# Two-layer hybrid decoder step: panel tiles in pieces, products without a reader, an opening on halves

## The chip, the cores and the metric

The kernel runs on one core of one Trainium2 chip. The metric is the device time of one execution in microseconds (us), median of three runs.

## The reference, cut to what matters

Two layers, 256 prompt tokens and 32 sample tokens (8 sequences of 4) with the same weights, all in float32. Each layer projects x (288 tokens x 1024) on 3592 columns, gives them to four recurrent head groups (RG-LRU, mLSTM, retention, HGRN2, 4 heads of 64 each), and projects their outputs back:

```python
proj = einsum('btd,de->bte', x, w_in[l])               # 14 groups of 256 columns and 8 gate columns
ya, yb, yc, yd = rglru(..), mlstm(..), retention(..), hgrn2(..)   # chunked recurrences, new states
x = layer_norm(ALPHA * x + concat(ya, yb, yc, yd) @ w_out[l])
# layer 0: swiglu, 1024 -> 2816 -> 1024; layer 1: top 2 of 8 experts, 1024 -> 1408 -> 1024
x = layer_norm(ALPHA * x + ffn(x))
```

The outputs are x of both groups of tokens and all new states.

## The kernel before, in words

The kernel is one program of five instruction streams, each written out by hand in its order, tied by semaphores. x lies in SBUF transposed, 8 blocks of 128 channels x 288 tokens. A **panel** is 256 columns of a weight matrix (1 MB), loaded by SP's queue into one of eleven slots; w_in has 14 panels a layer, which alternate between slots 0 and 1. A panel gives two **tiles** of 128 columns x 288 tokens; a tile is 8 products of TensorE (one for each block of channels) that accumulate in bank 0 or 1 of PSUM. Each float32 product has two records in the trace.

A **mixing stage** (`mix(l)` in TensorE's stream) computes the 28 tiles in the order FD QD KB QB XA VB KC QC ID VC GA GD GC OB. Between the tiles stand the small products of the four head groups: gate rows, the eight levels of HGRN2 (`level`), decays, scores, `outputs` (64-column heads, and one product of 4 columns for each sample sequence and head, `carried`), prompt states and sample states, means and variances of heads. ScalarE copies each tile out of PSUM (`in_ev`), VectorE computes the recurrences' elementwise parts in its own fixed order, and a `need(name, step)` lets an engine wait for a named step of another. Banks 2 and 3 (`A_`), 4 and 5 (`B_`), 6 and 7 (`C_`) are shared by the small products. Of the names that come up later: `m5`, `l6` are merge 5 and the operands of level 6 on VectorE, `ml_dv y` is its copy of mLSTM's outputs with the three operations behind it, `hg_dv y` and `ret_dv y` the same for the others; GpSimd spreads the values for the sample states (`vm_ready`).

**The opening** (layer 0). SP's queue loads the gate weights, x's first half (blocks 0 to 3), panel 0, x's second half, small tables, panel 1, large tables. GpSimd's queue loads the columns (small vectors), the LRU weights and three states. TensorE runs the gate products, tile 0, gate rows, tile 1. VectorE computes constants from the columns (lines 1553 to 1584), then copies the gate products (line 1912) and goes on with `gate_bias`, `forget` and so on to the operands of level 0.

**After the second mixing stage** stands the routing: layer norm of x in two halves of tokens (`mean`, `variance`), the products of the router (`logit_parts`), transposes of x to rows (`x_rows`), selection of experts on VectorE, positions of the tokens (products with `before` and `ones`), and `first_tokens`, which gathers the first expert's tokens by one-hot products. Then each of the 8 experts has an up part (16 steps over W1 and W3, 384 records) and a down part (264 records).

Line 583 is `mm`, the helper of all products, 586 is `tr`, a transpose as a product with the identity; 1286 is the helper of all of ScalarE's operations.

## Time and profile before

| what | value |
|---|---|
| median of 3 runs | 1114.41 us (1111.52 to 1116.57) |
| the profiled execution | 1113.72 us |
| its span, first to last instruction | 1111.9 us |
| mean granted clock of TensorE | 0.969 |
| TensorE matmul / weight load busy | 1071.3 / 758.2 us |
| VectorE / ScalarE / GpSimd busy | 324.0 / 170.2 / 74.7 us |
| HBM traffic | 228.60 MB read, 13.07 MB written |

By stages, in us from the span's start: opening to 22, mixing stage of layer 0 to 194, output projection and dense feed-forward to 505, mixing stage of layer 1 to 678, output projection and routing to 744, experts to 1095, combination and last norm to the end. A view in order of time merges instructions of one kind that follow each other: start, time, engine, line, operation, output <- inputs, rows x columns, number, and in brackets how long the engine had been idle before and what ended that. Busy times of TensorE are those of a pipeline: the differences of starts are used for what a piece of work takes.

### The profile page before, as it was taken

To read this page: it belongs to the slowest core of one execution; us is meant where nothing else is said; L and a number is where in the kernel's file an instruction comes from. 1 tells how busy PE (TensorE), PEld (TensorE's weight loads), DVE (VectorE), ACT (ScalarE), POOL (GpSimd) and SP (SyncE) were. 2 spreads that over 40 slices of the span, in tenths; PEclk is the share of its full clock that TensorE was granted. 3 is DMA by queue.
4 is the path that set the end of the run, shared out by engine and by line. 5 is a ranking of instruction groups with operands and counts; after the bars stand their busy time and mean duration, and the time that the engine had idled before them with its cause. 6 is when DMAs were issued, how large, how long until landed. Compare 5 with 4: busy or idle time off the path is not lost.

```text
span 1111.9 us, 20901 instructions
## 1 busy us (share of the span) xinstructions
PE 1071.3 (96%) x9627; PEld 758.2 (68%) x9627; DVE 324.0 (29%) x686; ACT 170.2 (15%) x360; POOL 74.7 (7%) x94
## 2 busy tenths in 40 slices
PE   6999999999999999999999999889999999999995
PEld 4787766897777777897876766733566566566552
DVE  4645535240000000137546443441110110110116
ACT  1322223130000000024222222220000000000011
POOL 1000113000000000000010300030000020000001
PEclk9998999999999999999998989959999999999998
DMA  8342147303433612403422335769999999999944
GB/s 340 114 190 77 39 135 261 152 11 142 151 151 124 263 49 104 185 1 104 185 92 75 101 119 230 281 228 385 363 402 418 401 409 397 423 421 423 408 151 131
DMA packets 36252, 240.06 MB, mean 216 GB/s; under 512 B 4736, under 2 KB 8064, under 8 KB 16320
## 3 DMA queue, kind: packets, MB, share of 16 engines
q1 hardware_dynamic: 26608, 216.40, 49.5%
q0 software_dynamic: 6416, 19.52, 5.1%
q10 hardware_dynamic: 3136, 2.75, 0.8%
q8 instruction: 77, 1.26, 0.5%
q14 instruction: 15, 0.12, 0.0%
HBM read 228.60 MB, written 13.07 MB: 217 GB/s over the span
## 4 chain that ended last, share of the span: by engine, by line
PE 94%; DVE 3%; ACT 1%; DMA 1%; issue 1%; SPq 0%; DVEq 0%
PE ps L583 93%; PE ps L586 1%; DMA x<-in_x 1%; ACT overlay L1286 1%; ACT L1286 0%; DVE overlay L1620 0%; DVE up_slots L1720 0%; ACT up_slots L1286 0%; DVE tables L2136 0%; DVE overlay L2019 0%; DVE up_slots L1959 0%; DVE up_slots L1713 0%; DVE up_slots L1960 0%; DVE tables L2143 0%; ACT x L1286 0%
## 5 line engine op out<-in xcount | busy, mean ns | idle before, releaser
L583 PE MATMUL ps<-x,up_slots 128*128 128x288 f32 (+2 forms) x1696 | 411.1, 402 | 0.9 <-ACT x L1286 0.8
L583 PEld LDWEIGHTS ps<-x,up_slots 128*128 128x128 f32 x1696 | 314.3, 194 | 89.4 <-issue 8.4
L583 PE MATMUL ps<-up_slots,mix_or_moe 128*32 128x352 f32 (+2 forms) x3248 | 253.0, 458 | 2.9 <-issue 1.6
L583 PEld LDWEIGHTS ps<-up_slots,mix_or_moe 128*32 128x32 f32 (+2 forms) x3248 | 126.5, 113 | 119.7 <-issue 25.6
L583 PE MATMUL ps<-overlay,up_slots 128*128 128x288 f32 (+2 forms) x824 | 150.9, 344 | 2.7 <-DVE overlay L2052 1.5
L583 PEld LDWEIGHTS ps<-overlay,up_slots 128*128 128x128 f32 x824 | 128.0, 191 | 25.4 <-DVE overlay L2052 2.0
L583 PE MATMUL ps<-overlay,tables 128*32 128x256 f32 (+4 forms) x1988 | 124.0, 376 | 4.9 <-DVE overlay L1614 2.5
L583 PEld LDWEIGHTS ps<-overlay,tables 128*32 128x32 f32 (+2 forms) x1988 | 86.4, 114 | 40.4 <-issue 3.6
L1286 ACT ACTIVATE overlay<-ps 128x288 f32<-128x288 f32 (+3 forms) x77 | 33.4, 434 | 412.4 <-PE ps L583 412.4
L2166 DVE TENSOR_TENSOR mix_or_moe<-mix_or_moe,ps 128x352 f32<-128x352 f32 x24 | 11.1, 517 | 196.3 <-PE ps L583 196.3
L510 POOL TENSOR_TENSOR up_slots<-mix_or_moe,tables 32x2048 f32<-32x2048 f32 x6 | 21.7, 3620 | 573.8 <-ACT mix_or_moe L1286 573.8
L2052 DVE TENSOR_TENSOR overlay<-overlay,ps 128x576 f32<-128x576 f32 x11 | 8.3, 754 | 156.1 <-ACT overlay L1286 156.1
L1588 DVE SCALAR_TENSOR_TENSOR x<-x,ps 128x576 f32<-128x576 f32 (+2 forms) x17 | 9.8, 577 | 105.5 <-PE ps L583 105.5
L1286 ACT ACTIVATE tables<-ps 128x256 f32<-128x256 f32 (+2 forms) x27 | 9.9, 430 | 198.0 <-PE ps L583 192.1
L2174 DVE STREAM_TRANSPOSE tables<-mix_or_moe 128x352 f32<-128x352 f32 x21 | 15.9, 808 | 77.2 <-PE ps L583 77.2
L1286 ACT ACTIVATE mix_or_moe<-ps 128x352 f32<-128x352 f32 (+3 forms) x39 | 15.6, 461 | 148.6 <-PE ps L583 147.6
L1286 ACT ACT_TABLE_LOAD x29 | 37.2, 1283 | 3.1 <-issue 1.8
L583 PE MATMUL ps<-up_slots 128*32 128x256 f32 (+2 forms) x520 | 35.0, 328 | 1.8 <-issue 1.3
L583 PEld LDWEIGHTS ps<-up_slots 128*32 128x32 f32 (+2 forms) x520 | 24.8, 148 | 13.6 <-issue 8.1
L1286 ACT ACTIVATE overlay<-x 128x512 f32<-128x512 f32 (+1 forms) x12 | 8.1, 683 | 133.3 <-DVE x L1608 133.3
L554 POOL DMA_DIRECT2D mix_or_moe<-expert_tokens x28 | 16.2, 588 | 153.7 <-DVE mix_or_moe L2157 151.3
L1860 DVE TENSOR_TENSOR up_slots<-overlay,up_slots 128x256 f32<-128x256 f32 (+1 forms) x14 | 11.9, 851 | 34.8 <-ACT up_slots L1286 34.8
(278 smaller groups left out, 592.9 us busy)
## 6 DMA issues: line engine op xcount, KB each, us to landing
up_slots<-in_moe_w SPq DMA_DIRECT2D x64, 1408.0 KB, 15.3
overlay<-in_moe_w SPq DMA_DIRECT2D x21, 1536.0 KB, 16.2
up_slots<-in_ffn_w SPq DMA_DIRECT2D x30, 1024.0 KB, 7.0
up_slots<-in_w_in SPq DMA_DIRECT2D x28, 1024.0 KB, 4.9
up_slots<-in_w_out SPq DMA_DIRECT2D x8, 1024.0 KB, 9.0
overlay<-in_moe_w SPq DMA_DIRECT2D x7, 1024.0 KB, 19.9
up_slots<-in_moe_w SPq DMA_DIRECT2D x3, 1536.0 KB, 16.4
...
```

Source lines behind the costliest of these rows:

```text
L510: pool.tensor_tensor(vm, VT[0:NS, 2, kind * 256:kind * 256 + 256].rearrange("p (h v) -> p h v", h=NH) .unsqueeze(2).to_broadcast([NS, NH, ...
L554: pool.dma_start(XGT[e % 2][GT * q:GT * q + GT], src[q]).then_inc(S[f"xgt_in_{e % 2}"], 16)
L583: return pe.matmul(o, lhsT, rhs, start=start, stop=stop)
L586: return pe.transpose(o, src, ident[0:k, 0:k])
L1286: return act.activation(o, i, fn, **kw)
L1588: stt(x2, x2, ALPHA, PS[:, bank:bank + 2, c], M, AD).then_inc(evicted, 1)
L1860: tt(qo[1], q[1], x[1], M)
L2052: tt(hid[:, 2 * n:2 * n + 2, :], sil[:, 2 * h:2 * h + 2], PS[:, 4 * h + 2:4 * h + 4, 0:T], M).then_inc(S["ffn_h"], 1)
L2166: tt(h, h, PS[:, 3 * ((e + 1) % 2) + g, 0:CH], M).then_inc(S["moe_h"], 1)
L2174: v.transpose(ht[:, g], HID[e % 2][:, g].rearrange("p (q i) -> p i q", i=FT)).then_inc(S["ht_done"], 1)
```

## The change

- **Pieces.** `tile_piece(i, k0, k1)` runs products k0 to k1 of tile i. Tiles 15, 16, 22 and 23 of each mixing stage are no longer run whole, but in pieces of one to four products between the parts of `outputs`, the prompt states, the sample states and HGRN2's outputs. `outputs` and `sample_states` take the pairs of heads that they run. Products, operands and sums stay the same.
- **Products without a reader.** `spin(n, bank)` runs n products of 128 x 288 of two tables into a bank that nobody reads before it is written again: 4 and 4 around the second variance of the last mixing norm, one before the selection's products, one behind the last `x_rows`, two before the first expert. In the opening six products of 256 columns on ones run before the gate products; VectorE writes the ones first.
- **Opening.** Panel 0 is loaded in two halves (channel blocks 0 to 3, and 4 to 7), with x's second half between them. TensorE runs, for each half, the gate products and the halves of tiles 0 and 1. GpSimd's queue waits for the large tables before it loads the LRU weights and the states. VectorE's series for the LRU constant moves from before the copy of the gate products to behind it, in two parts, one ahead of `gate_bias` and one ahead of `forget`.

The diff, cut to its core:

```diff
@@ -386,9 +386,14 @@
                 for i, tile in enumerate(ORDER):
                     if i >= 2:
                         sp.wait_ge(S["in_ps"], N_IN * l + 2 * i - 2)
-                    refill(i % 2, ("in", l, i), w_in[l][i])
                     if l == 0 and i == 0:
+                        sp.dma_start(UP[:, 0, 0:1024], w_in[0][0][:, 0:1024]).then_inc(S["first_panel_in"], 16)
                         x_half_in(1)
+                        loaded["in", 0, 0] = loaded["n", 0] = 16
+                        sp.dma_start(UP[:, 0, 1024:2048], w_in[0][0][:, 1024:2048]).then_inc(full[0], 16)
+                    else:
+                        refill(i % 2, ("in", l, i), w_in[l][i])
+                    if l == 0 and i == 0:
                         sp.dma_start(TB[:, 0:P], tab[:, 0:P]).then_inc(S["early_tables_in"], 16)
                         sp.dma_start(TB[:, late_tb:], tab[:, late_tb:]).then_inc(S["early_tables_in"], 16)
                     if l == 0 and i == 1:
...
@@ -501,6 +506,8 @@
                     pool.wait_ge(S["lru_ps"], l)
                     for e in range(NE):
                         pool.dma_start(XG[CAP * e:CAP * e + CAP, :], tab[0:CAP, 0:D]).then_inc(S["xg_zeroed"], 16)
+                else:
+                    pool.wait_ge(S["tables_in"], 16)
                 pool.dma_start(LW[:, :, :, :], A["lru_w"][l].rearrange("p (r a n) -> p r a n", r=2, a=2)).then_inc(S["lru_in"], 16)
                 if l:
                     pool.wait_ge(S["states_stored"], 16 * STORES * l)
...
@@ -513,7 +520,6 @@
                         tb("batchmask").unsqueeze(1).unsqueeze(3).to_broadcast([NS, NH, NB, HD]),
                         ALU.mult).then_inc(S["vm_ready"], 1)
 
-                pool.wait_ge(S["tables_in"], 16)
                 pool.wait_ge(*mark("ml_ac", "vt", l))
                 values(VM_ML, 0)
                 pool.wait_ge(*mark("lru_dv", "out", l))
...
@@ -585,6 +591,10 @@
             def tr(o, src, k):
                 return pe.transpose(o, src, ident[0:k, 0:k])
 
+            def spin(n, bank):
+                for _ in range(n):
+                    mm(PS[:, bank, 0:T], tb("lnmean"), tb("cos"))
+
             def mean(q, h, evicted, count):
 
                 c = HALVES[h]
...
@@ -636,19 +646,27 @@
                     if cols[-1].stop == T:
                         last.then_inc(S["in_ps"], 1)
 
+                def tile_piece(i, k0, k1):
+                    if k0 == 0:
+                        if i % 2 == 0:
+                            pe.wait_ge(full[i // 2 % 2], loaded["in", l, i // 2])
+                        pe.wait_ge(S["in_ev"], N_IN * l + i - 1)
+                    w = slot(i // 2 % 2)
+                    for k in range(k0, k1):
+                        last = mm(PS[:, i % 2, 0:T], w[:, k, i % 2 * P:i % 2 * P + P], X[:, k], k == 0, k == KT - 1)
+                    if k1 == KT:
+                        last.then_inc(S["in_ps"], 1)
+
                 def rows_of(h):
                     return HD * (h % 2), h // 2
 
                 def tokens(t):
                     return P if t < 2 else NS
 
-                def gates(c=slice(0, T)):
+                def gates(c):
                     pe.wait_ge(S["gate_weights_in"], 16 * (l + 1))
                     for k in range(KT):
-                        if l:
-                            x_half(1, HALVES.index(c), k)
-                        elif k % 4 == 0:
-                            pe.wait_ge(S[f"x_in_{k // 4}"], 16)
+                        x_half(1, HALVES.index(c), k)
                         j = k % NH
                         last = mm(PS[HR * j:HR * j + HR, A_, c], WG[:, k, :], X[:, k, c], k < NH, k >= NH)
                     if c.stop == T:
...
@@ -772,13 +790,15 @@
                     mm(o, key(buf, 0, 2 * p + h), rhs(0, 2 * p + h), True, False)
                     return mm(o, key(buf, 1, 2 * p + h), rhs(1, 2 * p + h), False, True)
 
-                def sample_states(bank, buf, vm, nth, name):
-                    pe.wait_ge(S["vm_ready"], 3 * l + nth)
-                    for p in range(2):
+                def sample_states(bank, buf, vm, nth, name, pairs=(0, 1)):
+                    if 0 in pairs:
+                        pe.wait_ge(S["vm_ready"], 3 * l + nth)
+                    for p in pairs:
                         for h in range(2):
                             last = mm(PS[HD * h:HD * h + HD, bank + p, :], key(buf, 2, 2 * p + h),
                                       vm[:, 2 * p + h].rearrange("p b v -> p (b v)"))
-                    end(last, name, "states")
+                    if 1 in pairs:
+                        end(last, name, "states")
 
                 def level(e, bank):
                     if e < NL - 1:
...
@@ -833,11 +853,28 @@
                     end(last, name, "rb")
 
                 if l == 0:
-                    gates()
-                    proj_tile(0)
-                    pe.wait_ge(S["early_tables_in"], 32)
-                    gate_rows()
-                    proj_tile(1)
+                    ones = PFIN.rearrange("p k a v -> p (k a v)")
+                    pe.wait_ge(S["spin_ready"], 1)
+                    for _ in range(6):
+                        mm(PS[:, B_, 0:256], ones[:, 0:P], ones[:, P:P + 256])
+                    pe.wait_ge(S["gate_weights_in"], 16)
+                    for h, sem in enumerate((S["first_panel_in"], full[0])):
+                        ks = range(4 * h, 4 * h + 4)
+                        pe.wait_ge(S[f"x_in_{h}"], 16)
+                        for k in ks:
+                            j = HR * (k % NH)
+                            last = mm(PS[j:j + HR, A_, 0:T], WG[:, k, :], X[:, k], k < NH, k >= NH)
+                        if h:
+                            end(last, "gate_ps", "gates")
+                        pe.wait_ge(sem, 16)
+                        for b in range(2):
+                            if h and b:
+                                pe.wait_ge(S["early_tables_in"], 32)
+                                gate_rows()
+                            for k in ks:
+                                last = mm(PS[:, b, 0:T], slot(0)[:, k, b * P:b * P + P], X[:, k], k == 0, k == KT - 1)
+                            if h:
+                                last.then_inc(S["in_ps"], 1)
                 else:
                     first, second = HALVES
                     gates(first)
...
@@ -891,22 +928,28 @@
                 need("ml_dv", "qs")
                 need("ml_dv", "keys")
                 pe.wait_ge(S["s0_in"], 48 * (l + 1))
-                outputs(B_, 0, value(0), state(0), QH[:, 0])
+                outputs(B_, 0, value(0), state(0), QH[:, 0], (0,))
+                tile_piece(15, 0, 2)
+                outputs(B_, 0, value(0), state(0), QH[:, 0], (1,))
+                tile_piece(15, 2, 4)
                 end(denominators(C_), "ml_ps", "out")
                 level(5, A_)
-                proj_tile(15)
+                tile_piece(15, 4, 8)
                 need("hg_dv", "m5")
                 level(6, A_)
                 need("ml_dv", "y")
                 for p in range(2):
+                    tile_piece(16, 3 * p, 3 * p + 3)
                     for h in range(2):
                         r = slice(HD * h, HD * h + HD)
                         prompt_state(PS[r, C_, p * HD:p * HD + HD], value(0), 0, p, h)
                         prompt_state(PS[r, C_, P + p:P + p + 1], lambda t, n: onesc[:, 0:1], 0, p, h)
                         last = mm(PS[r, C_, P + 8 + 8 * p:P + 16 + 8 * p], key(0, 2, 2 * p + h), tb("batchmask"))
                 end(last, "ml_ps", "pstate")
-                sample_states(B_, 0, VM_ML, 1, "ml_ps")
-                proj_tile(16)
+                sample_states(B_, 0, VM_ML, 1, "ml_ps", (0,))
+                tile_piece(16, 6, 7)
+                sample_states(B_, 0, VM_ML, 1, "ml_ps", (1,))
+                tile_piece(16, 7, 8)
                 need("hg_dv", "m6")
                 level(7, A_)
                 need("ml_dv", "states")
...
@@ -959,19 +1002,24 @@
                     for h in range(2):
                         mm(o[h][:, SEQ:T], value(2)(2, 2 * p + h), ATs[:, 2 * p + h], True, False)
                     last = carried(o, p, state(2), XB[0][:, :, SEQ:T])
+                    if p == 0:
+                        tile_piece(22, 0, 4)
                 end(last, "hg_ps", "out")
-                proj_tile(22)
+                tile_piece(22, 4, 8)
                 need("ret_ac", "vt")
                 need("ret_dv", "qs")
-                end(outputs(A_, 1, value(1), state(1), QH[:, 1]), "ret_ps", "out")
+                outputs(A_, 1, value(1), state(1), QH[:, 1], (0,))
+                tile_piece(23, 0, 3)
+                end(outputs(A_, 1, value(1), state(1), QH[:, 1], (1,)), "ret_ps", "out")
+                tile_piece(23, 3, 6)
                 need("hg_dv", "y")
                 sample_states(B_, 0, VM_HG, 2, "hg_ps")
+                tile_piece(23, 6, 8)
                 need("ml_dv", "n")
                 for p in range(2):
                     for h in range(2):
                         last = prompt_state(PS[HD * h:HD * h + HD, C_, p * HD:p * HD + HD], value(1), 1, p, h)
                 end(last, "ret_ps", "pstate")
-                proj_tile(23)
                 need("ret_dv", "y")
                 sample_states(A_, 1, VM_RET, 3, "ret_ps")
                 need("hg_dv", "states")
...
@@ -1092,7 +1140,9 @@
             mean(2, 1, S["out_x"], 2 * HALF_OUT)
             x_rows(0, 0)
             x_rows(0, 1)
+            spin(4, 4)
             variance(2, 1)
+            spin(4, 4)
             for k in range(KT):
                 x_half(2, 1, k)
                 last = logit_parts(1, k)
...
@@ -1104,6 +1154,8 @@
             last.then_inc(S["logits_ps"], 1)
             for i in range(2):
                 x_rows(1, i)
+            pe.wait_ge(S["xtk_done"], 2)
+            spin(1, 2)
             pe.wait_ge(S["sel_done"], 1)
             sel = SEL.rearrange("p t e -> p (t e)")
             mm(PS[:, 0, 0:3 * NE], tb("before"), sel, True, False)
...
@@ -1115,6 +1167,7 @@
             last.then_inc(S["count_ps"], 1)
             for i in range(2):
                 x_rows(2, i)
+            spin(1, 2)
 
             def first_tokens():
                 pe.wait_ge(S["xtk_done"], 6)
...
@@ -1204,6 +1257,7 @@
 
             with pe.If(sparse):
                 pe.sem_inc(S["ln_room"], 1)
+                spin(2, 2)
                 for e in range(NE):
                     a, b = (0, 3) if e % 2 == 0 else (3, 0)
                     pe.wait_ge(S["xe_done"], e + 1)
...
@@ -1545,6 +1599,7 @@
             M, AD, SU, MX, MN = ALU.mult, ALU.add, ALU.subtract, ALU.max, ALU.min
 
 
+            v.memset(PFIN[:, :, :, :], 1.0).then_inc(S["spin_ready"], 1)
             v.wait_ge(S["columns_in"], 16)
             lam = vec["lru_lambda"]
             e_, z, y2, pl, t0 = (N0S[:, 4 * i:4 * i + 4] for i in range(5))
...
@@ -1582,6 +1622,27 @@
             ts(LC[:, 4:8], d2, 1e-30, None, MX)
             link(ts(LC[:, 8:12], d2, -1.0, 1.0, M, AD))
             link(v.memset(SM[:, :], 0.0))
+
+            def series():
+                link(ts(t0, e_, 2.0, None, AD))
+                link(v.reciprocal(t0, t0))
+                link(tt(z, e_, t0, M))
+                link(tt(y2, z, z, M))
+                link(ts(pl, y2, 1.0 / 19, 1.0 / 17, M, AD))
+                for n in (15, 13, 11, 9):
+                    link(tt(pl, pl, y2, M))
+                    link(ts(pl, pl, 1.0 / n, None, AD))
+
+            def decay_const():
+                for n in (7, 5, 3, 1):
+                    link(tt(pl, pl, y2, M))
+                    link(ts(pl, pl, 1.0 / n, None, AD))
+                link(tt(pl, pl, z, M))
+                link(ts(t0, lam, -1.0, 0.0, M, MX))
+                link(stt(t0, pl, 2.0, t0, M, AD))
+                link(ts(LC[:, 0:4], t0, -4.0, None, M))
+                for name in ("lru_br", "lru_bi"):
+                    link(ts(vec[name], vec[name], 0.5, None, M))
 
             def residual(m, c, bank, evicted):
                 x2 = X[:, 2 * m:2 * m + 2, c]
...
@@ -1910,7 +1971,11 @@
                     v.wait_ge(S["levels_zeroed"], 1)
                 need("gate_ps", "gates")
                 end(cp(gsb, PS[:, 2, 0:T]), "gate_dv", "gsb")
+                if l == 0:
+                    series()
                 gate_bias()
+                if l == 0:
+                    decay_const()
                 forget()
                 queries()
                 link(v.memset(ATALL, 0.0))
```

## Rows read from the trace of the kernel before

**Rows 1.** The page: TensorE's busy time, and the clock granted in 40 slices.

```profile
PE 1071.3 (96%) x9627; PEld 758.2 (68%) x9627; DVE 324.0 (29%) x686; ACT 170.2 (15%) x360; POOL 74.7 (7%) x94
...
PEclk9998999999999999999998989959999999999998
```

**Rows 2.** Stretches: window, us, busy of five engines (instructions), clock, DMA share, GB/s.

```profile
94.30:101.20 6.90, 6.90 (x69) 5.09 (x68) 2.30 (x7) 0.00 (x0) 0.00 (x0) 0.51 0.01 2
...
719.00:725.80 6.80, 4.34 (x23) 2.69 (x21) 3.89 (x10) 2.96 (x9) 0.00 (x0) 0.50 0.03 12
...
729.20:749.80 20.60, 18.58 (x136) 7.25 (x140) 7.13 (x31) 3.94 (x5) 11.10 (x14) 0.50 0.68 255
```

**Rows 3.** TensorE's timeline around tile 15, first layer, then second.

```profile
94.51 1.77 PE L583 MATMUL ps<-mix_or_moe,tables 128*32 128x256 f32 x24
...
103.98 1.34 PE L583 MATMUL ps<-up_slots 64*128 64x64 f32 x24
...
581.00 1.05 PE L583 MATMUL ps<-mix_or_moe,tables 128*32 128x256 f32 x24
...
583.45 4.15 PE L583 MATMUL ps<-x,up_slots 128*128 128x288 f32 x16
...
587.53 1.34 PE L583 MATMUL ps<-up_slots 64*128 64x64 f32 x24
```

**Rows 4.** TensorE's timeline: sample states and tile 16, then the third sample states, first layer.

```profile
108.13 1.11 PE L583 MATMUL ps<-up_slots,mix_or_moe 32*64 32x512 f32 x1
...
117.43 1.41 PE L583 MATMUL ps<-overlay 64*128 64x128 f32 x24
...
172.34 1.93 PE L583 MATMUL ps<-up_slots,mix_or_moe 32*64 32x512 f32 x8
```

**Rows 5.** The timeline: six tiles in a run, from tile 1 on.

```profile
18.67 23.44 PE L583 MATMUL ps<-x,up_slots 128*128 128x288 f32 x96
```

**Rows 6.** VectorE's timeline after level 5, second layer.

```profile
585.28 0.43 DVE L1861 TENSOR_TENSOR up_slots<-overlay,up_slots 128x288 f32<-128x288 f32 x1
...
587.40 0.46 DVE L1796 TENSOR_TENSOR overlay<-overlay 128x288 f32<-128x288 f32 x1
```

**Rows 7.** Opening: TensorE's timeline, then level 0 and VectorE, then a group by line.

```profile
5.17 1.19 PE L583 MATMUL ps<-x,gate_weights 128*32 128x288 f32 x8 [5.17 <-DMA x<-in_x]
...
10.55 1.19 PE L583 MATMUL ps<-x,gate_weights 128*32 128x288 f32 x8 [4.20 <-DMA x<-in_x]
...
11.66 6.19 PE L583 MATMUL ps<-x,up_slots 128*128 128x288 f32 x16
...
41.16 0.42 DVE L1861 TENSOR_TENSOR up_slots<-overlay,up_slots 128x256 f32<-128x256 f32 x1
...
42.04 1.11 PE L583 MATMUL ps<-up_slots 64*128 64x64 f32 x16
...
L1566 DVE TENSOR_SCALAR tmp_small<-tmp_small 128x4 f32<-128x4 f32 x8 | 1.4, 170 | 0.3
```

**Rows 8.** TensorE's timeline from the second variance on, with the experts' first parts.

```profile
718.54 2.11 PE L583 MATMUL ps<-overlay,tables 128*128 128x160 f32 x8 [2.47 <-DVE overlay L1614]
...
723.11 2.90 PE L583 MATMUL ps<-x,columns 128*32 128x160 f32 x16 [2.46 <-ACT x L1286]
...
729.22 1.75 PE L583 MATMUL ps<-small,tables 128*128 128x24 f32 x12 [0.93 <-DVE small L2097]
...
730.90 1.89 PE L586 MATMUL ps<-tables,x 128*32 128x128 f32 x8
...
733.46 8.95 PE L583 MATMUL ps<-tables,mix_or_moe 128*32 128x256 f32 x72 [0.68 <-ACT tables L1286]
...
743.74 31.53 PE L583 MATMUL ps<-up_slots,mix_or_moe 128*32 128x352 f32 x384 [1.33 <-DVE mix_or_moe L2178]
...
776.84 28.61 PE L583 MATMUL ps<-up_slots,mix_or_moe 128*32 128x352 f32 x384 [1.56 <-issue]
...
1062.35 14.45 PE L583 MATMUL ps<-overlay,tables 128*32 128x256 f32 x264
```

20 lines of the change are left out of this document (3 added, 17 removed).

## The prediction

> **What bounds the kernel now.** I read the page first: TensorE's matmul row is busy in 96% of the span, and the row of the granted clock is under full in five places [rows 1]. So the time is what TensorE does, and a wait of another engine counts only where TensorE has to stand for it. There are then three ways to make this kernel shorter: fewer idle gaps of TensorE (some 40 us in all, 10 of them before its first full stretch of work), less work, or the same work at a higher clock. The change removes no work. So I asked next for the clock in stretches [rows 2]: in the two mixing stages there are five stretches of about 6.85 us at half clock (1.2 GHz instead of 2.4), all alike, of which the first stands in the rows; between the second mixing stage and the experts there are two more, one of 6.8 and one of 20.6 us, and in the first of these TensorE works in 4.3 us only. TensorE is "busy" in every one of the five, so the busy share hides the loss. What the engine did just before each fall is seen in its timeline: before 94.3 and 162.6 the products of outputs() (32 records of 4 columns among few of 256), before 108.0 and 592.7 the prompt states, before 647.3 outputs() and products on 32 rows; before 719 and 729.2 waits and transposes. Full tiles of a panel never stand before a fall, and a full tile ends each of the five.
>
> **What half clock costs in the mixing stages.** The same stretch (denominators, level 5, tile 15) ran at half clock in the first layer and at full clock in the second: from 94.51 to 103.98 it is 9.47 us, from 581.00 to 587.53 it is 6.53, so 2.94 us lost [rows 3]. The second stretch (sample states, tile 16) runs from 108.13 to 117.43, 9.30 us; at full clock the sample states took 1.93 (their third set, at 172.34) [rows 4] and a tile 4.08 (583.45 to 587.53) [rows 3], sum 6.01: 3.29 lost. The three others have the same length and the same make-up (sample states and a full tile) and are not shown; I take 3.2 each. Sum: 2.94 + 3.29 + 3 x 3.2 = 15.8 us, near the bound that half of 5 x 6.85 gives, 17.1.
>
> **Part 1, the pieces.** Tiles 15, 16, 22 and 23 are cut so that two to four full products of 288 columns stand between the small ones. All four were there already, so no column is added. *Removed:* the 15.8 us, if no stretch falls any more. After the change the longest run of small products between two pieces is half of outputs(), about 2.1 us, or the prompt states of a pair (1.5 us) with one pair's sample states (0.9). Before, over 4 us of such work stood together. The weakest place is that last one: 1.5 + 0.9 us of narrow work, then a single product of tile 16 (0.5), then 0.9 again. *Added (a):* a piece costs an entry. A tile alone takes 4.08 from start to start [rows 3]; six in a run take 23.44, 3.91 each [rows 5]; an entry is so 0.15 to 0.2. There are eight more pieces a layer (2 + 3 + 1 + 2), 16 in all: 2.4 us. Bounds: 0 (the small products lose an entry for each) and 3.2. *Added (b):* a wait that is hidden today. After level 5, VectorE merges, forms the operands of level 6 and then copies out mLSTM's outputs. In the second layer level 5 ended at 583.45; the operands were done at 585.28 + 0.43, and the last instruction of the outputs (ml_dv y) at 587.40 + 0.46, so 2.3 and 4.4 us later [rows 6]. Today the whole tile 15 (4.08) lies between; then only its last four products do (2.05). TensorE comes to level 6 0.3 early, runs it (1.3) and comes to "y" at 3.6, 0.9 early. Queued behind it are tile 16's first piece, the prompt and the sample states, the whole rest of the stage. 1.2 us a layer, 2.4 in all; bounds 0 and 3. The tiles' own conditions (the bank emptied by ScalarE two tiles ago) are met long before. The wait on VectorE at the second swap (1.2 us a layer) stays: it hangs on tile 16's end and on what VectorE does after, and both move together. Net of part 1: 15.8 - 2.4 - 2.4 = 11.0 us.
>
> **Part 2, the opening.** Now x's first half lands at 5.17, the second at 10.55, after the whole of panel 0 [rows 7]. TensorE does 1.2 us of gate products at each and then tile 0 at 11.66, at half clock at first: 16 records in 6.19 us, against 3.91 at full clock, 2.2 us lost. Tile 1 ends at 18.67 + 3.91 = 22.6. After: six products of 256 columns on ones, from about 1.3 us, take 6 x 0.85 = 5.1 us at half clock and end at about 6.4; they lie in the wait for x. Panel 0's first half (0.5 MB) was not split before; by the pace at which x and panel 0 landed (1.6 MB from 5.17 to 10.55, with the state loads beside them, which now wait for the tables) it lands at about 6.8, x's second half at 8.5, the panel's second at 10. TensorE then has: gates 0.6 to 1.2 (to 7.3), eight products 3.9 (to 11.3, with 0.2 for the clock), gates 0.6, four products 1.95, gate rows 1.0, four products 1.95: 16.9. That is 5.7 before today's 22.6. Then VectorE is next. It had level 0's operands at 41.16 + 0.42 and TensorE took them at 42.04 [rows 7], a slack of only 0.45. Its chain doesn't move up as much: the 27 small instructions of the series, 0.2 us each (eight pairs of them in the row at 0.17), move from before the gates' copy to behind it, half of them ahead of gate_bias and half ahead of forget(), where they are now on the way: gates copied at 12.4, series to 15.0, bias to 16.5, rest to 19.3, against 23.19 today for forget(); of its 18.4 us up to level 0 some 1.1 were waits for ScalarE that go. That gives 36.6, and TensorE comes at 16.9 + 5 x 3.91 = 36.5. So both are there together, and the gain at 42.04 is 5.4 us; I take 5.3. Bounds: 2.2 (the clock alone, if halves land as today) and 6.5. GpSimd's queue: the LRU weights and three state loads now stand behind the tables' landing (24.2 today); their first readers are at 84 and 90 us. SP's: panel 2 is issued at 17 instead of 22.7 behind the tables, and has until 24.8; hidden, or up to 1 us late.
>
> **Part 3, products without a reader.** They stand in five waits. The 2.47 us before the variance (718.54) and the 2.46 after it (723.11) get four products of 288 columns each, 4 x 0.49 = 1.96 at full clock: both fit [rows 8]. The wait before the selection's products gets one, the one after its transposes one, and two go before the first expert. If the clock then stays at full: the variance takes 1.05 instead of 2.11 (1.0), the selection and the transposes 1.75 + 1.89 become some 1.2 + 1.1 (1.3; so the chain to the first tokens is 2.3 shorter, and VectorE's one-hot rows, which hang on the selection, come earlier too). The first tokens: 72 records in 8.95 us at half clock; 264 records of the same shape took 14.45 in an expert's down product, so 72 are 3.9; I take 4.3, 4.6 won. The first expert's up: 31.53 us against 28.61 for the same 384 records of the second, 2.9. Against that, VectorE isn't ready sooner at the end than it can transpose, and two products (0.98) stand in a wait of 1.33 that shrinks: 0.8 back. 1.0 + 1.3 + 4.6 + 2.9 - 0.8 = 9.0 us. Bounds: 0.5 and 10.
>
> A rule speaks against this part. The row at 730.90 is eight transposes, and such transposes stand before both falls of this stage. The Trainium skill (TensorE: Matmul & The Clock Gate, Part 4, PE-mode transpose) says that transposes through TensorE don't count as its activity for the full clock. By that, the single products would be too little around the selection and the clock would fall as today; this trace doesn't contradict it. It is rival 1.
>
> **The sum.** 11.0 + 5.3 + 9.0 = 25.3 us. The profiled execution took 1113.72 (span 1111.9 and 1.8 around it), so 1088.4 for it; it lies 0.7 under the median of the three runs, 1114.41, so I forecast 1089. The memory traffic of the experts is near its limit, but their weights' loads are released by TensorE's own steps and move up with them.
>
> **Rivals.**
> 1. *The clock still falls at the selection* and the first tokens and the first up run at half clock as now. For it: the transposes above, and only 0.5 us of product in each gap. Against: the waits in between are filled. Part 3 gives 1.0 (the variance), less 0.5 for the last two products, which at half clock (1.92) overrun their 1.33. Time: 1114.4 - 11.0 - 5.3 - 0.5 = 1097.6. Chance 0.25.
> 2. *A mixing stage still falls*, at the prompt and sample states of tile 16, where the pieces are smallest. Price 3.3 for one layer, 6.6 for both: 1092 to 1096. For it: the run named above. Chance 0.2.
> 3. *The clock doesn't follow what TensorE does* (the falls have another cause), so nothing is won by filling. Then the products without a reader run at half clock, 3.84 us in waits of 2.47, 1.4 over each, with 0.9 more at the three others: +3.7. The pieces and the new wait cost 4.8, and the opening gains 3.1 (5.3 without its 2.2 of clock): 1114.4 + 3.7 + 4.8 - 3.1 = 1119.8, slower. It decides as soon as a filled wait shows half clock. Against it: every fall comes after thin work or a wait and none within the 180 us of full tiles. Chance 0.03.
> 4. *The halves don't land earlier*: the opening gives 2.2, and the rest holds: 1092. Chance 0.07.
>
> **How the numbers follow.** The forecast has 0.45: 1089, between 1085 (entries and the wait free) and 1092. The range takes in the first rival whole: 1084 to 1098. Below lie a few per cent (all bounds at their best), above the third rival and mixtures of the first and second. 0.5% is about what a measurement of this kernel can tell from no change, here 5.6 us; all cases but the third and a worst mixture are faster by more: 0.94 faster, 0.03 within, 0.03 slower.
>
> **What would show each step right or wrong.** In the changed kernel's stretches the clock reads full from 90 to 120, 160 to 170 and at the same places of the second layer; if one reads 0.5, it should be at the states of tile 16. TensorE's list of waits has new ones at level 6 and at the first piece of tile 16, on VectorE, together 1.2 us a layer. Level 0 starts at about 36.6 instead of 42.04. The variance takes 1.05 us, the first tokens 4.3, the first up 28.6. The prediction is wrong where a stretch of half clock comes up at a new place, or where VectorE's shifted series holds TensorE at level 0 by more than 1 us.

## The result, and the profile after

The changed kernel takes 1097.78 us (median of 4 runs, 1095.82 to 1098.93); the kernel before took 1113.61 beside it (1111.52 to 1116.57). The ratio is 0.9845 [0.9817, 0.9874], so it is 1.55% faster, by 14 to 20 us. The forecast was 1089 in 1084 to 1098: the sign held, and the time lies just inside the upper end of the range, 8.8 us over the forecast. The profiled execution took 1095.82 (span 1093.9), 17.9 under the profiled one of before, where 25.3 had been forecast.

The page, TensorE's row and the clock in 40 slices (in [rows 1] there are 8s and a 5 short of the last slice, here none):

```profile
PE 1061.0 (97%) x9663; PEld 752.5 (69%) x9663; DVE 323.6 (30%) x687; ACT 170.0 (16%) x360; POOL 75.2 (7%) x94
...
PEclk9999999999999999999999999999999999999998
```

Windows of the changed kernel: stretch, length, busy time of TensorE, its weight loads, VectorE, ScalarE and GpSimd (instructions), granted clock, DMA share, GB/s:

```profile
90.00:120.00 30.00, 27.88 (x241) 19.80 (x238) 20.20 (x47) 6.00 (x10) 0.00 (x0) 1.00 0.22 71
160.00:170.00 10.00, 10.00 (x60) 6.38 (x61) 7.37 (x11) 5.05 (x7) 7.11 (x14) 1.00 0.89 266
572.00:602.00 30.00, 27.88 (x221) 19.66 (x220) 21.13 (x48) 5.99 (x10) 0.00 (x0) 1.00 0.21 71
640.00:655.00 15.00, 15.00 (x90) 9.18 (x90) 8.74 (x13) 6.69 (x10) 2.71 (x5) 1.00 0.48 153
490.70:494.10 3.40, 3.40 (x15) 2.48 (x14) 0.58 (x2) 0.75 (x3) 0.00 (x0) 0.51 0.00 0
726.20:729.70 3.50, 2.76 (x20) 0.99 (x24) 1.63 (x3) 0.00 (x0) 0.68 (x1) 0.51 0.04 7
```

The first four are where the five falls of the mixing stages stood before [rows 2]: full clock now. Two short falls of 3.4 us stand outside them, at 490.7 (a wait for x in the second layer's beginning) and 726.2 (the first expert).

TensorE's timeline at level 6 and tile 16, first layer, then second (start, time, engine, line, operation, shapes, number, idle before and what ended it):

```profile
94.20 2.21 PE L589 MATMUL ps<-x,up_slots 128*128 128x288 f32 x8
96.60 1.34 PE L589 MATMUL ps<-up_slots 64*128 64x64 f32 x24 [0.20 <-DVE up_slots L1922]
98.65 1.72 PE L589 MATMUL ps<-x,up_slots 128*128 128x288 f32 x6 [0.71 <-DVE overlay L1857]
...
577.65 1.34 PE L589 MATMUL ps<-up_slots 64*128 64x64 f32 x24 [0.20 <-DVE up_slots L1922]
579.70 1.72 PE L589 MATMUL ps<-x,up_slots 128*128 128x288 f32 x6 [0.71 <-DVE overlay L1857]
```

The two new waits of part 1 stand where they were forecast, 0.20 and 0.71 us in each layer. The opening, in the same view:

```profile
1.33 5.17 PE L589 MATMUL ps<-prompt_states 128*128 128x256 f32 x12 [1.33 <-DVE prompt_states L1602]
6.43 0.69 PE L589 MATMUL ps<-x,gate_weights 128*32 128x288 f32 x8
7.79 4.15 PE L589 MATMUL ps<-x,up_slots 128*128 128x288 f32 x16 [0.66 <-DMA up_slots<-in_w_in]
...
37.00 1.11 PE L589 MATMUL ps<-up_slots 64*128 64x64 f32 x16
```

The gates and tile 0 now run at full clock (8 gate products in 0.69 against 1.19, 16 of tile 0 in 4.15 against 6.19 [rows 7]), and level 0 starts at 37.00 with no wait before it, against 42.04. The routing, TensorE's timeline:

```profile
704.21 1.35 PE L589 MATMUL ps<-overlay,tables 128*128 128x160 f32 x8 [0.53 <-DVE overlay L1675]
...
713.92 1.13 PE L589 MATMUL ps<-small,tables 128*128 128x24 f32 x12 [0.44 <-DVE small L2162]
714.98 1.05 PE L592 MATMUL ps<-tables,x 128*32 128x128 f32 x8
...
716.75 5.67 PE L589 MATMUL ps<-tables,mix_or_moe 128*32 128x256 f32 x70 [0.23 <-ACT tables L1340]
723.20 0.59 PE L589 MATMUL ps<-tables,mix_or_moe 32*32 32x256 f32 x2 [0.78 <-issue]
724.62 1.13 PE L589 MATMUL ps<-tables 128*128 128x288 f32 x4 [0.84 <-issue]
726.94 3.31 PE L589 MATMUL ps<-up_slots,mix_or_moe 128*32 128x352 f32 x24 [1.19 <-DVE mix_or_moe L2243]
...
758.43 1.98 PE L589 MATMUL ps<-up_slots,mix_or_moe 128*32 128x352 f32 x24 [1.56 <-issue]
```

Against [rows 8]: the variance 1.35 for 2.11, the selection 1.13 for 1.75, its transposes 1.05 for 1.89, the first tokens 5.67 for 8.95. But the first up follows 10.19 after the tokens' start, where it was 10.28: TensorE stands for 0.78, 0.84 and 1.19 us in between. What the first up waits for is seen in VectorE's and GpSimd's timelines (at the end of a row: "issue", nothing that the profile shows; "remote", a queue or core that it doesn't know):

```profile
721.92 0.45 DVE L2243 STREAM_TRANSPOSE mix_or_moe<-ps 128x256 f32<-128x256 f32 x1 [1.52 <-issue]
726.11 0.78 DVE L2243 STREAM_TRANSPOSE mix_or_moe<-ps 128x256 f32<-128x256 f32 x2 [3.73 <-remote]
...
717.51 1.06 POOL L553 DMA_INDIRECT expert_tokens<-tables,slot_index  x1 [70.88 <-ACT tables L1340]
...
723.87 0.85 POOL L553 DMA_INDIRECT expert_tokens<-tables,slot_index  x1 [0.30 <-issue]
```

VectorE transposes the first of three groups of tokens and then stands from 722.37 to 726.11, 3.73 us, ahead of the other two. GpSimd issues its six indirect transfers (the **scatter** of the tokens for the other experts) from 717.51 to 724.72.

The trace's record of the semaphores says which side is late. VectorE waits for one signal of TensorE for each group. Counted from the tokens' start, the last product of the second group ends at 3.20 us in TensorE's records (whose ends are modelled), its signal is recorded at 9.33, and VectorE starts 0.03 later; the third group ends at 7.03, its signal comes at 9.56. So it isn't VectorE that is slow: the signals come 6.1 and 2.5 us after the recorded ends. (Since these ends are modelled, it stays open whether only the signals were late or the products too.)

By anchors in TensorE's timeline, profiled executions, in us. "Mixing" runs from level 0 to the first product of the out-projection:

| part | before | after | won | forecast |
|---|---|---|---|---|
| start to level 0 | 42.04 | 37.00 | 5.04 | 5.3 |
| mixing, first layer | 152.54 | 145.80 | 6.74 | 7.0 |
| out-projection to second half of the gates, layer 2 | 306.56 | 306.56 | 0 | 0 |
| from there to level 0 | 27.45 | 28.68 | -1.23 | 0 |
| mixing, second layer | 149.58 | 145.80 | 3.78 | 4.0 |
| to the first tokens | 55.29 | 52.91 | 2.38 | 2.3 |
| first tokens to first up | 10.28 | 10.19 | 0.09 | 3.8 |
| first up to the second's | 33.10 | 31.49 | 1.61 | 2.9 |
| rest | 335.06 | 335.47 | -0.41 | 0 |
| sum (span) | 1111.9 | 1093.9 | 18.0 | 25.3 |

(Forecast by layer: three falls, 2.94 + 3.29 + 3.2, less 2.4, is 7.0; two of 3.2 less 2.4 is 4.0. First tokens: 4.6 - 0.8.) Of the 7.3 us that are missing 3.7 stand in one row.

### The profile page after: what moved, and what is told of

The parts are those of the page before. It is cut to its first block, busy times and chain, and to the rows that moved or that the text cites. A ratio compares the mean times of both kernels' runs of the same rounds, so it can differ in the third digit from the quotient of the medians.

```text
span 1093.9 us, 20975 instructions
## 1 busy us (share of the span) xinstructions
PE 1061.0 (97%) x9663; PEld 752.5 (69%) x9663; DVE 323.6 (30%) x687; ACT 170.0 (16%) x360; POOL 75.2 (7%) x94
## 3 DMA queue, kind: packets, MB, share of 16 engines
q10 hardware_dynamic: 3136, 2.75, 0.8%
## 4 chain that ended last, share of the span: by engine, by line
PE 91%; DVE 4%; ACT 2%; DMA 1%; issue 1%; POOL 0%; another core or an unknown queue 0%; ACTq 0%; DVEq 0%; POOLq 0%; SPq 0%
PE ps L589 90%; PE ps L592 1%; DMA overlay<-expert_rows,slot_index 1%; ACT overlay L1340 1%; DMA up_slots<-in_w_in 1%; ACT L1340 1%; POOL overlay L576 0%; DVE overlay L1681 0%; DVE up_slots L1781 0%; ACT up_slots L1340 0%; DVE tables L2201 0%; ACTq L1562 0%; ACT tables L1340 0%; DMA expert_rows<-tables 0%
## 5 line engine op out<-in xcount | busy, mean ns | idle before, releaser
L589 PE MATMUL ps<-x,up_slots 128*128 128x288 f32 (+2 forms) x1696 | 406.2, 397 | 2.9 <-DVE overlay L1857 1.4
L589 PEld LDWEIGHTS ps<-x,up_slots 128*128 128x128 f32 x1696 | 307.1, 191 | 88.1 <-issue 9.8
L589 PE MATMUL ps<-up_slots,mix_or_moe 128*32 128x352 f32 (+2 forms) x3248 | 246.8, 453 | 2.7 <-issue 1.6
L589 PEld LDWEIGHTS ps<-up_slots,mix_or_moe 128*32 128x32 f32 (+2 forms) x3248 | 123.8, 112 | 117.8 <-issue 23.5
```

The source lines that it names most:

```text
L589: return pe.matmul(o, lhsT, rhs, start=start, stop=stop)
```

## The experiments

The experiments' medians, each with its ratio to the kernel before in the same series, are in us. They were measured in three series, and the changed kernel itself in none of them: kernels of different series are compared by their ratios.

**Theory.** The parts do what was forecast, and the first tokens' gain is lost to something that holds VectorE. **Rivals.** The parts depend on each other; or the clock falls with the position, not with what TensorE does.

**1. One part at a time.** Part 1 alone (only_pieces), on the kernel before:

```diff
-outputs(B_, 0, value(0), state(0), QH[:, 0])
+outputs(B_, 0, value(0), state(0), QH[:, 0], (0,))
+tile_piece(15, 0, 2)
+outputs(B_, 0, value(0), state(0), QH[:, 0], (1,))
+tile_piece(15, 2, 4)
...
```

> The kernel before with part 1 alone (tiles 15, 16, 22 and 23 in pieces). Theory: the five stretches of half clock in the mixing stages go and two short waits on VectorE per layer come, as the changed kernel's trace shows: its two mixing stages are 6.7 and 3.8 us shorter, so about 10.5 us less than before, 1103. Rival (the falls are spread by the rest of the change, not by the pieces): some of the five stretches stay, each costs 3.3 us, and the time is 1106 or more.

Measured: 1105.08 (1103.79 to 1105.79), ratio 0.9923 [0.9897, 0.9950], that is 5.6 to 11.5 us less. Mixing took 145.80 in the first layer, as in the whole change, and 147.46 in the second, where one fall was left:

```profile
592.00:599.00 7.00, 7.00 (x35) 4.17 (x34) 3.84 (x8) 3.16 (x6) 0.00 (x0) 0.53 0.00 0
```

It costs 1.66 us and not the 3.3 of [rows 4]. Most of the difference is a wait that it swallows: after tile 16 the changed kernel stands 1.22 us for VectorE, and only_pieces, coming late, doesn't. TensorE's timeline, the changed kernel, then only_pieces (four products, a wait and four more; then eight without one):

```profile
597.97 1.24 PE L589 MATMUL ps<-overlay,tables 128*128 128x288 f32 x4 [1.22 <-DVE overlay L1956]
```

```profile
591.85 1.47 PE L583 MATMUL ps<-up_slots,mix_or_moe 32*64 32x512 f32 x4
...
602.98 2.10 PE L583 MATMUL ps<-overlay,tables 128*128 128x288 f32 x8
```

The clock goes down in the row at 591.85 (four products of the sample states, 1.47 for 1.07): that is the place which rival 2 named. Whether it falls there isn't fixed by the code alone, since the changed kernel has the same rows and didn't. Part 2 alone (only_opening):

```diff
+for _ in range(6):
+    mm(PS[:, B_, 0:256], ones[:, 0:P], ones[:, P:P + 256])
...
+for h, sem in enumerate((S["first_panel_in"], full[0])):
```

> The kernel before with part 2 alone (halves of x and of panel 0, products on ones, moved series and loads). Theory: level 0 starts at 37.0 instead of 42.04 and nothing after it gives the 5.0 us back, about 1108.6. Rival (later falls of the clock depend on where the stages stand in time, so a shift alone moves the total): the gain differs from 5.0 by a multiple of some 1.2 to 3.3 us, with a stretch of half clock at a place where before has none.

Measured: 1110.19 (1104.71 to 1113.31), ratio 0.9974 [0.9946, 1.0002]. In its trace level 0 starts at 37.17, 4.9 earlier than before, so the part does its work; in the time only 2.9 us show, with an interval from none to 6.0, which holds the 4.9 and doesn't prove them. The trace answers the rival of the position. In the five traces whose tiles are all whole (before, this one, and three below) the second layer's two falls stand 64.0 to 64.1 and 118.6 to 118.8 us after that layer's level 0, though level 0 itself moves by 14 us between them (519.6 here, 528.6 before). There they follow the code and not the time. In the first layer they differ from trace to trace, and it costs 147.95 here and 152.54 before with the same code in it.

Part 3 alone (only_routing):

```diff
+spin(4, 4)
 variance(2, 1)
+spin(4, 4)
...
```

> The kernel before with part 3 alone (twelve products without a reader in five waits of the routing). Theory: the clock stays full up to the first tokens, these take 5 to 6 us less on TensorE, but VectorE's transposes behind its branch end the wait as late as before, so only about 4 us are won, 1109.5. Rival (my prediction's sum): the first tokens' gain comes through and 9 us are won, 1104.6.

Measured: 1112.79 (1107.79 to 1116.09), ratio 0.9990 [0.9970, 1.0009]. Its stage is 2.38 shorter up to the tokens (52.91), as in the whole change, then 10.14 to the first up, nothing won, and 32.63 to the second's, 0.5 won. Neither the 4 us of the theory nor the rival's 9 show in the time; the interval, 3.3 us less to 1.0 more, just holds the 3.0 of these three rows. Its profiled execution had a mixing stage of 155.89 in the first layer, 3.35 more than before with none of that stage's code changed: 27.2 us of it at half clock for 20.4. 20 runs of the kernel before in this series lie between 1108.36 and 1119.83.

The three parts alone are worth 8.6, 2.9 and 1.1 us by their ratios, 12.6 together, where the whole change won 17.3. Their intervals are wide enough for the difference, so that the parts depend on each other is neither shown nor excluded.

**2. What holds the first up.** VectorE branches after routing, and its transposes stand behind the branch. If the branch holds them, they should come sooner ahead of it (early_transposes):

```diff
+for g in range(NG):
+    v.wait_ge(S["oh_ps"], g + 1)
+    last = v.transpose(XE[0][:, :, GT * g:GT * g + GT], ...)
+last.then_inc(S["xe_done"], 1)
 sparse = v.value_load(FLAG[0:1, 0:1], min_val=0, max_val=1)
```

> The changed kernel, in which VectorE makes its three transposes of the first expert's tokens ahead of its branch and not behind it. In the changed kernel's trace the first transpose comes 1.5 us after the branch and the second 3.7 us after the first, though the tokens were long there. Theory (VectorE is late because it has just branched): the first up starts when TensorE's two products end, at about 725.8 instead of 726.9, and the short fall of the clock behind it may go too (1.3 us): 1 to 2.5 us less than the changed kernel, about 1096. Rival (the transposes wait for TensorE's sums or for the one before them): the gap of 3.7 us stays, only in another place, and the time stays at 1097.8.

Measured: 1096.80 (1095.70 to 1098.28), ratio 0.9849 [0.9816, 0.9883]: no gain. VectorE's timeline:

```profile
720.76 0.45 DVE L2196 STREAM_TRANSPOSE mix_or_moe<-ps 128x256 f32<-128x256 f32 x1
726.36 0.78 DVE L2196 STREAM_TRANSPOSE mix_or_moe<-ps 128x256 f32<-128x256 f32 x2 [5.15 <-remote]
```

The first group is transposed 3.69 after the tokens' start (717.07) instead of 5.17, with no branch ahead of it, and the second waits all the same, now 5.15. The branch isn't it. The next candidate is the scatter, since 726.36 is 1.3 after its last issue, nearly as in the changed kernel (723.87 + 0.85 to 726.11: 1.39). GpSimd's issues were put behind VectorE's transposes (late_scatter):

```diff
 pool.wait_ge(S["idx_ready"], 1)
+pool.wait_ge(S["xe_done"], 1)
 for t in range(3):
```

> The changed kernel, in which GpSimd's six indirect DMAs (the tokens' rows to memory) wait until VectorE has made the first expert's three transposes. In the changed kernel they run at the same time as the first tokens, and VectorE's second transpose comes 1.3 to 1.5 us after the last of them ends, in all traces so far, however fast TensorE was. Theory (the scatter is what holds VectorE and TensorE there): TensorE's two short stops in and behind the first tokens go, the transposes are done at about 8 us after the first tokens began or earlier (now 10.1), and up to 2.5 us are won against the changed kernel, 1095.5. Rival (it is TensorE's sums or its two products that VectorE waits for): first tokens to first up stays at 10.1 and the time at 1097.8.

Measured: 1095.70 (1093.09 to 1098.80), ratio 0.9848 [0.9809, 0.9888]. TensorE's timeline, then VectorE's and GpSimd's:

```profile
717.50 4.76 PE L590 MATMUL ps<-tables,mix_or_moe 128*32 128x256 f32 x72 [0.23 <-ACT tables L1341]
...
723.36 1.09 PE L590 MATMUL ps<-up_slots,mix_or_moe 128*32 128x352 f32 x12
...
722.09 1.11 DVE L2244 STREAM_TRANSPOSE mix_or_moe<-ps 128x256 f32<-128x256 f32 x3 [1.04 <-issue]
...
724.06 1.06 POOL L554 DMA_INDIRECT expert_tokens<-tables,slot_index  x1 [76.67 <-DVE mix_or_moe L2244]
...
752.67 1.71 DVE L2223 STREAM_TRANSPOSE mix_or_moe<-mix_or_moe 128x256 f32<-128x256 f32 x3 [11.82 <-DMA mix_or_moe<-expert_tokens]
```

The tokens run without a stop (72 in 4.76, 3.9 to 4.3 had been forecast), the first up follows 5.86 after their start, 4.3 less. The second group's signal comes 0.04 us after its last product, and the transposes follow in a row. Yet the time gains at most 2 by the medians and nothing by the ratios (0.9848 and 0.9845): up to the second expert's it is now 32.96 for 31.49, and mixing had a fall in the second layer (147.45). And the scatter now meets the experts' weights: the second expert's tokens are transposed from 752.67 on instead of 735.23, 3.6 ahead of their reader (756.32). The same alone on the kernel before (before_late_scatter), and with part 3 alone (routing_and_late_scatter):

> The kernel before with the scatter after the transposes, nothing else. Theory: at half clock TensorE's own first tokens last till 742.4, 1.3 us before the first up, so moving the scatter away wins at most 0.5 us there and the time stays at 1112.7: the two edits are worth something only together. Rival (the scatter also slows TensorE's products at half clock): first tokens to first up is well under 10.2 us, and the time falls by 2 us or more.

> The kernel before with part 3 (products in the routing's waits) and the scatter after the transposes, nothing else. Part 3 alone won 1 us. Theory (the scatter hid what the full clock won in the first tokens): first tokens to first up takes 5.9 instead of 10.1 us, the stage from the mixing stage's end to the first tokens 52.9 instead of 55.3, the first up 29 to 30.5: some 7 to 8 us less than before, 1105 - which is near the 9.0 of my prediction. Rival (other losses hide it): 1109 or more.

Measured: 1115.99 (1111.95 to 1121.85), ratio 1.0052 [1.0029, 1.0075], and 1112.37 (1110.23 to 1117.21), 1.0014 [0.9993, 1.0035]. From the tokens to the first up it is 9.26 and 5.86; up to the second's 33.43 and 35.62. So with half clock the first tokens themselves (8.69) fill the time and 1.0 is won, with full clock 4.4. Both expectations of the time failed all the same: the first kernel is 3.9 us slower than the one before, clear of noise, and the second shows none of the 7 to 8 us. TensorE's timeline of the second kernel, ahead of the second expert's up:

```profile
771.28 28.93 PE L584 MATMUL ps<-up_slots,mix_or_moe 128*32 128x352 f32 x360 [7.01 <-issue]
```

It stands there 7.01 us for the second expert's tokens, 3.07 in before_late_scatter, and 1.5 to 1.6 in late_scatter and in all ten traces whose scatter isn't moved. Ahead of the last small products, near the end, TensorE stands 4.44 and 5.63 more for VectorE, and 0.33 in the kernel before; whether the moved scatter makes that too is open, since tile16_whole, measured in the same series with the scatter in its usual place, has 5.33 there. So an edit that frees 4.3 us at one wait gave 3.0 of them back at the next (35.62 for the 32.63 of only_routing).

**3. What keeps the clock.** The same pieces but tile 16 whole, after the sample states (tile16_whole):

```diff
 for p in range(2):
-    tile_piece(16, 3 * p, 3 * p + 3)
...
 sample_states(B_, 0, VM_ML, 1, "ml_ps", (0,))
-tile_piece(16, 6, 7)
 sample_states(B_, 0, VM_ML, 1, "ml_ps", (1,))
-tile_piece(16, 7, 8)
+tile_piece(16, 0, 8)
```

> The changed kernel with tile 16 in one piece behind the sample states, as in the kernel before; tiles 15, 22 and 23 stay in pieces. Theory (what runs between the small products decides whether the clock falls): one stretch of half clock at the states of tile 16 in each layer, 3.3 us each, less some 0.5 us of entries: 5 to 6 us more than the changed kernel, 1103. Rival (the pieces of tile 16 don't matter, the other cuts did it): no fall there, and the time is 1097 to 1098.

Measured: 1100.30 (1099.52 to 1102.31), ratio 0.9904 [0.9876, 0.9931]. The falls are back, in both layers, and the stages take 148.40 and 149.96 for 145.80:

```profile
104.50:111.50 7.00, 7.00 (x17) 3.75 (x14) 3.43 (x10) 0.00 (x0) 0.00 (x0) 0.51 0.01 4
585.50:596.50 11.00, 11.00 (x40) 6.97 (x40) 4.91 (x14) 0.57 (x1) 0.00 (x0) 0.53 0.03 10
```

The same columns in another order: it is the order that costs 2.6 and 4.2 us (2.5 in the second layer against the traces where the pieces left a fall). (TensorE is busy in all of both stretches.) By the ratios it is 6.6 us slower than the changed kernel, by the medians of two series 2.5; 5 to 6 had been expected. Of the profiled executions it is 4.3, since they differ elsewhere too, with the same code: level 0 starts 2.75 later here, the second layer's beginning takes 1.25 less and the rest 1.2 more, and from the first tokens to the second up it is 5.2 less. That last part is a surprise for the point before: the scatter stands where the changed kernel has it, and VectorE isn't held. TensorE's, VectorE's and GpSimd's timelines:

```profile
725.01 4.76 PE L589 MATMUL ps<-tables,mix_or_moe 128*32 128x256 f32 x72 [0.23 <-ACT tables L1338]
...
731.36 1.98 PE L589 MATMUL ps<-up_slots,mix_or_moe 128*32 128x352 f32 x24 [0.42 <-DVE mix_or_moe L2241]
...
730.19 1.11 DVE L2241 STREAM_TRANSPOSE mix_or_moe<-ps 128x256 f32<-128x256 f32 x3 [1.54 <-PE ps L589]
...
725.77 1.06 POOL L553 DMA_INDIRECT expert_tokens<-tables,slot_index  x1 [70.87 <-ACT tables L1338]
...
732.13 0.86 POOL L553 DMA_INDIRECT expert_tokens<-tables,slot_index  x1 [0.30 <-issue]
```

All three transposes in a row at 730.19, while GpSimd issues until 733.0; from the tokens to the first up it is 6.35. TensorE's signals come 0.04 us after the products here. In the nine other traces with the scatter in its usual place the second group's signal is recorded 9.26 to 9.44 us after the tokens' start, 1.3 to 1.5 after GpSimd's last issue; in the four with the late scatter it follows its product by 0.04. (That the 1.3 to 1.5 hardly vary proves little: GpSimd starts 0.76 after the tokens in all ten, so a fixed time after the tokens fits as well.) So the scatter in that place is a condition of the hold, not its whole cause.

Do transposes hold the clock as products do? In the gaps of part 3 (transposes_for_products):

```diff
-spin(4, 4)
+turn(9, 4)
 variance(2, 1)
-spin(4, 4)
+turn(9, 4)
...
-spin(1, 2)
+turn(2, 2)
```

> The changed kernel, in which four of its five fillings of the routing are transposes of about the same length in place of products without a reader: nine for each four products, two for each single one. If transposes count as little for the clock as my first rival took, it falls at the second variance or at the selection as in the kernel before (variance 2.1, first tokens 8.9 us) and the time is 2 to 4 us above the changed kernel's, 1100 to 1102. If they count like products, the variance takes 1.3, the first tokens 6 to 7 us, and the time stays at 1097.8.

Measured: 1098.72 (1097.20 to 1099.05), ratio 0.9863 [0.9831, 0.9895]. Windows:

```profile
707.00:717.00 10.00, 7.33 (x59) 5.02 (x57) 7.07 (x35) 4.13 (x11) 0.00 (x0) 1.00 0.49 183
717.00:730.80 13.80, 13.30 (x95) 4.45 (x96) 5.51 (x23) 3.45 (x5) 8.31 (x9) 0.51 0.71 272
```

TensorE's timeline of the same trace:

```profile
706.38 1.15 PE L592 MATMUL ps<-tables 128*128 128x128 f32 x9
...
714.90 1.13 PE L589 MATMUL ps<-small,tables 128*128 128x24 f32 x12 [0.70 <-DVE small L2166]
...
717.73 9.01 PE L589 MATMUL ps<-tables,mix_or_moe 128*32 128x256 f32 x72 [0.50 <-ACT tables L1344]
```

Variance and selection run as fast as with products (1.35, 1.13), 10 us past the first gap. Then the clock falls at 717, ahead of the tokens, which take 9.01; in none of the nine other traces with part 3 did it fall ahead of the tokens (in the changed kernel's at 726.2, after its stops). So the transposes are not nothing, since without any filling the clock fell just behind the first gap (719 in [rows 2]), and they may be less than products: they also leave 1.48 us idle where the products leave 0.52, and one trace can't tell these apart. Each expectation was met in half.

Four products in the wait for x, where the second layer begins (2.56 us; second_layer_products):

```diff
 variance(1, 1)
+spin(4, 4)
 gates(second)
```

> The changed kernel with four more products without a reader, in TensorE's 2.56 us wait for x at the beginning of the second mixing stage. There the changed kernel's trace has a stretch of half clock of 3.4 us that before's profiled execution hadn't, and this part took 28.7 instead of 27.45 us. Theory (that wait is a place where the clock can fall): 27.45 us again in each execution, 1.2 us or a little less against the changed kernel, 1096.7. Rival (four products cost what they save): no difference, 1097.8.

Measured: 1097.78 (1095.91 to 1100.16), ratio 0.9859 [0.9824, 0.9894]. The fall at 490.7 is gone (27.44 for 28.68), but it is gone without the products in late_scatter's trace too, and a fall at 587 came instead (147.45): nothing to see in the time.

**4. The wait that the pieces opened.** The first piece of tile 16 ahead of level 6, not behind it (tile16_earlier):

```diff
 tile_piece(15, 4, 8)
+tile_piece(16, 0, 3)
 need("hg_dv", "m5")
 level(6, A_)
 need("ml_dv", "y")
 for p in range(2):
-    tile_piece(16, 3 * p, 3 * p + 3)
+    if p:
+        tile_piece(16, 3, 6)
```

> The changed kernel with the first piece of tile 16 (three products) ahead of level 6 and not behind it. Theory (the two new waits on VectorE, 0.2 and 0.7 us in each mixing stage, cost TensorE their length): both go, and 1.8 us are won, 1096.0. Rival (the longer run of small products behind level 6 lets the clock fall there): a stretch of half clock at the states of tile 16 in some executions, 1.7 to 3.3 us each, and the time is 1097.8 or more.

Measured: **1093.91** (1092.47 to 1094.89), ratio 0.9825 [0.9793, 0.9858], the lowest of all, though its interval overlaps the changed kernel's. TensorE's timeline:

```profile
94.45 3.66 PE L589 MATMUL ps<-x,up_slots 128*128 128x288 f32 x14
98.05 1.34 PE L589 MATMUL ps<-up_slots 64*128 64x64 f32 x24
99.32 0.45 PE L589 MATMUL ps<-mix_or_moe 128*64 128x64 f32 x4
```

Both waits are gone, mixing takes 144.55 and 144.54, 1.25 less in each layer (0.91 of waits, and 0.34 that one entry less may explain), and no fall stands there in this trace. Last, this, late_scatter and second_layer_products in one (three_together):

> The changed kernel with three edits of the runs before together: the scatter after VectorE's transposes, the first piece of tile 16 ahead of level 6, four products in the wait of the second layer's beginning. If they add: first tokens to first up 5.9 instead of 10.2 us, each mixing stage 144.5, the second layer's beginning 27.4: against the changed kernel 4.3 - 1 (TensorE's stops that the scatter now makes during the first up) + 2 x 1.3 to 3.9 + up to 1.2, so 6 to 8 us less, 1090 to 1092. If the gains overlap (each had only removed the same fall of the clock), 1093 or more.

Measured: 1099.36 (1097.97 to 1100.16), ratio 0.9888 [0.9861, 0.9914]: not the 6 to 8 us less, and above each of the three, clear of noise only against tile16_earlier. A window of the first layer, then TensorE's timeline:

```profile
105.90:112.70 6.80, 6.80 (x34) 3.93 (x31) 3.43 (x7) 3.16 (x6) 0.00 (x0) 0.50 0.00 1
...
758.13 2.58 PE L590 MATMUL ps<-up_slots,mix_or_moe 128*32 128x352 f32 x16 [8.43 <-issue]
...
1083.75 2.78 PE L590 MATMUL ps<-mix_or_moe 32*32 32x256 f32 x24 [7.06 <-DVE small L2285]
```

The first up starts at 721.09, the earliest of all, and then TensorE stands 8.43 us for the second expert's tokens, since the scatter, issued until 729.0, landed at 742.8 among the loads of the experts' weights (in the changed kernel issued until 724.7, landed at 728.8). At the end it stands 7.06 more for VectorE, in the place where tile16_whole has 5.33.

It is not shown that the three edits spoil each other. routing_and_late_scatter has neither of the other two and waits 7.01 at the same place; counted from the tokens' start, the first up, GpSimd's issues and the next load of weights begin at the same times in both (5.86, 6.55 to 12.91, 9.68). late_scatter, of another series, differs in that TensorE stood 0.62 and 0.25 us inside its first up: the next load of weights was issued 1.24 us later there, the scatter landed 5 to 6 us sooner, and the wait was 1.52. So the late scatter wins or loses by a narrow margin. And the rival of tile16_earlier is seen in this trace: with the same order the clock falls at the states of tile 16 in both layers (105.9 and 587.2), and mixing takes 146.21 and 144.82.

## Why the prediction was right, and what it missed

The time fell inside the range by luck. Its upper end stands at 1098 only because rival 1 was taken in whole, and 1097.78 came by another way. Rival 2's highest price ends at 1096. By the prediction's own signs it is wrong in one more point: two falls came up at new places (490.7, 726.2).

**Part 1: right in the mechanism.** 15.8 for the falls less 4.8 makes 11.0; 6.74 + 3.78 = 10.5 was measured. The five falls went, and tile16_whole brings two back by the order alone. The new waits measured 0.91 a layer for 1.2. The entry was put at 0.15 to 0.2 us; tile16_earlier's 0.34 for one suggests more, though it isn't measured alone. That the "weakest place", the states of tile 16, would still fall (rival 2) wasn't so in the changed kernel's profile, but it was in the second layer of only_pieces, late_scatter, second_layer_products and transposes_for_products (147.45 or 147.46 each): four of the six traces with this order of pieces, though in the first layer of none. So rival 2 holds in some executions, at 1.65 and not at 3.3, mostly for the swallowed wait of 1.22 that its price left out.

**Part 2: right.** 5.04 for 5.3. Ones end at 6.4 as forecast, the panel's first half came at 7.8 instead of 6.8, and VectorE's chain and TensorE met at 37.0 (forecast 36.6). In tile16_whole the half came at 8.8 with a fall behind it, and level 0 at 39.75.

**Part 3, to the tokens: right.** 2.38 for 2.3. The variance took 1.35, not 1.05, and the selection with its transposes 2.18, not 2.3. Rival 1 (the clock still falls at the selection) named 1097.6, which is nearly the time that came, by a mechanism that didn't: the clock was full through selection, transposes and tokens. The rule of the Trainium skill behind it (TensorE: Matmul & The Clock Gate, Part 4, PE-mode transpose), that transposes don't count as activity, has the trace against it as far as the selection goes, and transposes_for_products doesn't refute it further on, where the clock fell at 717. A time that fits is no proof of a cause.

**The first tokens: the step that failed.** "4.3, 4.6 won" was right for TensorE's own work once it isn't held (4.76), and wrong as to what ends last. The step took 0.8 off for VectorE's transposes, and took for granted that these come as soon as TensorE's products are done. In the trace of before TensorE's tokens had ended 0.5 us ahead of the last transposes and GpSimd's last issue 1.46, and both fitted. But the second group's signal had come 3.6 us after its product there too (9.42 for 5.82, from the tokens' start), so the hold was in the trace already and half clock hid most of it. So 0.09 was won of 3.8. The runs show that without the scatter in that place it is 4.3, and that the 4.3 are not free: the scatter lands later, and TensorE then waits 1.5 to 8.4 us for the second expert's tokens. Why the signals come late there is open.

**The first up: 1.61 for 2.9.** A fall of 3.4 us at 726.2, right behind TensorE's stops, took the rest, so this is a result of the step before. In tile16_whole, where TensorE didn't stop in the tokens, the first up took 28.61, as forecast, and 30.16 to the second's, 2.94 less than before.

**Layer 2's beginning: -1.23, not in the sum.** A wait of 2.56 that was full-clock before had a fall behind it in this execution, as in early_transposes (28.72) and in part in only_opening (27.96); only_pieces, only_routing, late_scatter, tile16_earlier and tile16_whole have 27.44 or 27.45 there, as before. The sum left such falls out. **The rest:** the tail's -0.4, and the median lies 2 above the profiled execution. The forecast carried over the 0.7 that was seen on before; with falls that wander between executions that offset isn't a constant.

In sum: 3.7 (tokens) + 1.3 (first up) + 1.2 (layer 2) + 0.5 (mixing) + 0.3 (opening) + 0.4 (tail) - 0.1 = 7.3 us.
